# An empty first turn of the expert loop, transposes in two parts, no unused work at the tail, and 22 instead of 28 shared gate/up steps

## The chip, the cores and the metric

One core of one Trainium2 chip runs the whole program; the other cores are idle. The metric is the device time of one execution in microseconds (us), lower is better. All arithmetic is in float32. The engines are PE (matrix products; PEld is its loading of weights), DVE (elementwise), ACT (activation functions and copies), POOL (here mostly the starting of gathers and scatters) and SP (the starting of plain DMA transfers).

## The reference

The block has two halves over 1024 tokens of width 1024: a mixer (short convolution beside an RWKV-7 recurrence) and a mixture of experts. The change is in the second half, of which this is the core:

```python
def moe_ffn(xn, router_w, router_b, gu_w, gu_b, dn_w, dn_b):
    logits = xt @ router_w + router_b
    top_vals, top_idx = lax.top_k(logits, 4)          # of 32 experts
    gates = jax.nn.softmax(top_vals, axis=-1)
    ...                                               # tokens sorted by expert
    def expert_block(args):
        xb, e = args
        h = xb @ gu_w[e] + gu_b[e]                    # gate and up, 1024 -> 2 x 1024
        x_glu = jnp.minimum(h[:, 0::2], 7.0)
        x_lin = jnp.clip(h[:, 1::2], -7.0, 7.0)
        act = x_glu * jax.nn.sigmoid(1.702 * x_glu) * (x_lin + 1.0)
        return act @ dn_w[e] + dn_b[e]                # down, 1024 -> 1024
    ...                                               # times the gate, added at the token's row
y = rms_norm(h + moe_ffn(rms_norm(h, norm_ffn_w), ...), norm_final_w)
```

## The kernel before

The first half and the routing take the first 740 us of the span. The routing writes a list of tokens for each expert and, with DVE at L1484, a table `size_i` of one number for each expert: 1, 2 or 3, for up to 128, 144 or 160 tokens. Each engine then goes round its own loop over the experts; the engines meet only at semaphores. The order within an engine is the order of the code; nothing reorders it.

PE's loop is `expert_pe` (L2238 on). It is software pipelined by one expert: turn `t` finishes the down product of expert `t - 1` and then makes the gate/up product of expert `t`. In one turn PE issues:

- `down_first` (L2202): the down product is made with seven block products in place of eight (a Strassen scheme), in sums of quarters, and `down_first`, `down_second` and `down_third` are its stages. All share the helper `both` (L2194). DVE reads what a stage left in PSUM before the next stage may write there: L1549 (`y_first`) reads after `down_first`, and `down_second` waits for it; L1554 reads after `down_second`, and `down_third` waits for it.
- `transpose_tokens` (L2223 on): eight transposes of 128x128 (L2229) of the gathered tokens of the next expert into PSUM banks 4 and 5, and two (L2235) of the pieces of tokens 128 to 159 into bank 7. ACT copies these three to SBUF (`copy_xT`, L1019 and L1022) and counts `s_xe`.
- `down_second`, then `down_rest` (L2177, 32 small products for tokens 128 to 159) if the size is over 1, or `no_rest` (L2184, one dummy product) if it is 1, then `down_third`, of which the last part writes bank 6.
- `gate_up` (L2145): 128 steps, each one product of a 128x128 weight tile with 128, 144 or 160 tokens. In the code stand three copies: 100 steps with 160 tokens, 100 with 144, 122 with 128. Steps 100 to 121 stand once, with 160 tokens, for both larger sizes, and the last 6 once for all sizes. `WIDE` sets the first number. A float32 product of this kind shows as two matmul records and two weight loads in the trace.

The sizes reach PE's sequencer (the part of the engine that runs branches and hands matmuls to a queue) by `value_load`: register operations, a TENSOR_LOAD from `size_i`, and more register operations (L2240).

Before the loop PE issues 8 products on constants (`WARM`, L2131). After it the last expert's down product is made without the Strassen scheme (`down_half`, L2162), with a last set of transposes between its halves, of tokens that no expert uses. In step with that, POOL starts a last gather of such tokens (`gather(E, 0, E)` in `last_rows_out`) ahead of the load of the last expert's rows from `sum_s`, and ACT copies the transposes (`copy_xT(E)`).

In the tail DVE (`last_expert_dve`) takes the last expert's rows, adds the bias (L1594, L1595), makes from ACT's sums of squares (L1049) the scale of every token (L1597, ACT L1059, L1600), scales five of the eight output tiles (L1577; ACT scales three), and then handles the down product of the last expert. SP writes the eight tiles to `out` (L600), and when all have landed POOL scatters the last expert's rows over them (L753, L756).

`rounds` calls `expert_pe(0)`; its branch with a loop variable `r` is for experts with more than 160 tokens and is not entered with these inputs.

## Time and profile before

| | |
|---|---|
| median of 3 runs | 2271.7 us (2269.38 to 2271.95) |
| profiled execution, its own time | 2272.49 us |
| its span, first to last instruction | 2270.4 us |
| mean granted clock of PE | 0.990 |
| PE busy | 2200.7 us (97%) |
| DVE, ACT, POOL busy | 1259.6, 478.9, 350.2 us |
| the chain that ended last, by engine | PE 92%, DMA 3%, issue 2%, DVE 2% |
| of it the gate/up products (L2145) | 41% |
| of it the down products (L2194) | 17% |
| turns with a down part in the loop | 31 |
| transfers of kind "instruction" of 16 KB (queue q8) | 37, 0.61 MB |

The busy shares say that PE is hardly ever idle; the chain of waits goes through PE for 92% of the span. The granted clock is 1 at TensorE's full speed and 0.5 at half of it. "issue" as the cause of an idle time means that the engine waited for nothing that the profile shows. Queue q8 carries code to an engine.

### The profile page before, as it was taken

Reading aid. Unit: us, or ns where it says so; the run is one execution under the profiler, and the core shown is the slowest. Engines: PE = TensorE matmul, PEld = TensorE weight load, DVE = VectorE, ACT = ScalarE, POOL = GpSimd, SP = SyncE. Lnnn points to the kernel's source line nnn. Section 1 sums busy time; section 2 is a strip of 40 time slices with the busy share of each in tenths; the row PEclk is TensorE's granted clock in tenths of the full one; section 3 lists DMA queues with packets and bytes.
Section 4 is the critical chain, followed back from the end, with each engine's and each line's share of the span. In section 5 each row is a group of like instructions: output and inputs, shape, how many; then the busy total and the mean of one; then the engine's idle time right before and its main releaser. Section 6 shows DMA issues by size and latency. Waiting matters only on the chain.

```text
span 2270.4 us, 49537 instructions
## 1 busy us (share of the span) xinstructions
PE 2200.7 (97%) x19222; PEld 1600.0 (70%) x19223; DVE 1259.6 (55%) x2504; ACT 478.9 (21%) x988; POOL 350.2 (15%) x360
## 2 busy tenths in 40 slices
PE   8999998899999998999999999999999999999997
PEld 3444444888445776888678877788777887788775
DVE  6466533455434455556655665556655665556664
ACT  3233001444333111111111111111111111111113
POOL 0000001121022211111112211122111221121112
PEclk9999999999998999999999999999999999999998
DMA  3111112333533767888878988689877998679987
GB/s 143 50 60 47 51 61 64 96 104 123 192 131 104 310 254 279 304 301 309 333 272 298 344 303 308 253 324 340 307 301 263 333 350 325 254 292 334 349 300 260
DMA packets 120628, 535.01 MB, mean 236 GB/s; under 512 B 27795, under 2 KB 61735, under 8 KB 87776
## 3 DMA queue, kind: packets, MB, share of 16 engines
q1 hardware_dynamic: 98416, 489.30, 56.2%
q0 software_dynamic: 22160, 44.98, 7.8%
q8 instruction: 37, 0.61, 0.1%
q14 instruction: 15, 0.12, 0.0%
HBM read 485.24 MB, written 40.05 MB: 231 GB/s over the span
## 4 chain that ended last, share of the span: by engine, by line
PE 92%; DMA 3%; issue 2%; DVE 2%; POOL 0%; ACT 0%; SPq 0%; POOLq 0%; DVEq 0%
PE ps L2145 41%; PE ps L2194 17%; PE ps L1654 9%; PE ps L1752 5%; PE ps L2025 5%; PE ps L2177 2%; PE ps L1851 2%; PE ps L2229 1%; PE ps L1701 1%; PE ps L1860 1%; DMA idx_g<-list_s 1%; PE ps L1833 1%; PE ps L1865 1%; DMA arena<-xn_s,idx_g 1%; PE ps L1953 1%
## 5 line engine op out<-in xcount | busy, mean ns | idle before, releaser
L2145 PE MATMUL ps<-arena 128*128 128x128 f32 (+2 forms) x8192 | 994.2, 284 | 10.3 <-issue 8.9
L2145 PEld LDWEIGHTS ps<-arena 128*128 128x128 f32 x8192 | 986.2, 192 | 22.9 <-issue 21.2
L2194 PE MATMUL ps<-arena 128*64 128x512 f32 x1984 | 393.3, 544 | 9.9 <-DVE arena L1554 9.7
L1508 DVE TENSOR_TENSOR arena<-arena 128x1024 f32<-128x1024 f32 x248 | 294.3, 1217 | 0.0
L2194 PEld LDWEIGHTS ps<-arena 128*64 128x64 f32 x1984 | 134.2, 137 | 218.9 <-issue 193.9
L1495 DVE TENSOR_SCALAR arena<-ps,arena 128x160 f32<-128x160 f32 x256 | 97.9, 382 | 321.3 <-PE ps L2145 320.0
L1027 ACT ACTIVATE arena<-arena 128x160 f32<-128x160 f32 x256 | 86.1, 336 | 815.9 <-DVE arena L1495 815.9
L1654 PE MATMUL ps<-arena 128*128 128x512 f32 x448 | 195.7, 594 | 0.0
L730 POOL DMA_INDIRECT sum_s<-arena,idx_s x31 | 51.5, 1662 | 851.9 <-ACT arena L1042 851.9
L1654 PEld LDWEIGHTS ps<-arena 128*128 128x128 f32 x448 | 84.5, 190 | 109.4 <-issue 109.4
L1752 PE MATMUL ps<-arena 128*128 128x512 f32 x280 | 120.6, 592 | 0.8 <-ACT arena L871 0.8
L2025 PE MATMUL ps<-arena 128*128 128x512 f32 x256 | 113.7, 594 | 0.0
L1499 DVE SCALAR_TENSOR_TENSOR arena<-arena 128x160 f32<-128x160 f32 x256 | 83.3, 325 | 49.1 <-ACT arena L1027 48.1
L1752 PEld LDWEIGHTS ps<-arena 128*128 128x128 f32 x280 | 53.1, 190 | 68.1 <-issue 68.1
L1496 DVE TENSOR_SCALAR arena<-ps,arena 128x160 f32<-128x160 f32 x256 | 95.8, 374 | 0.0
L714 POOL DMA_INDIRECT arena<-xn_s,idx_g x33 | 39.6, 1200 | 351.7 <-DMA idx_g<-list_s 336.1
L1502 DVE TENSOR_TENSOR arena<-arena 128x160 f32<-128x160 f32 x256 | 83.2, 325 | 8.8
L2025 PEld LDWEIGHTS ps<-arena 128*128 128x128 f32 x256 | 47.6, 190 | 55.2 <-issue 54.9
L1554 DVE TENSOR_TENSOR arena<-ps,arena 64x512 f32<-64x512 f32 x31 | 21.2, 684 | 108.7 <-PE ps L2194 108.7
L1042 ACT ACTIVATE arena<-arena,idx_s 128x512 f32<-128x512 f32 x62 | 44.8, 722 | 145.1 <-DVE arena L1567 140.2
L1851 PE MATMUL ps<-arena 64*64 64x64 f32 x1328 | 56.9, 224 | 7.7 <-issue 5.3
L1561 DVE TENSOR_TENSOR arena<-ps,arena 64x512 f32<-64x512 f32 x31 | 21.2, 684 | 77.1 <-PE ps L2194 77.1
(280 smaller groups left out, 2088.6 us busy)
## 6 DMA issues: line engine op xcount, KB each, us to landing
arena<-gu_w SPq DMA_DIRECT2D x128, 2048.0 KB, 11.5
arena<-dn_w SPq DMA_DIRECT2D x128, 1024.0 KB, 11.2
arena<-dn_b SPq DMA_DIRECT2D x32, 512.0 KB, 15.4
arena<-w_in_t SPq DMA_DIRECT2D x26, 512.0 KB, 3.2
arena<-arena SPq DMA_DIRECT2D x50, 256.0 KB, 2.7
arena<-w_out SPq DMA_DIRECT2D x2, 2048.0 KB, 7.9
arena<-x SPq DMA_DIRECT2D x8, 512.0 KB, 5.1
xn_s<-arena SPq DMA_DIRECT2D x8, 512.0 KB, 2.8
```

What stands on the lines that cost most here:

```text
L1027: nc.scalar.activation(sgm[f % 2], gt[f % 2], ACT.Sigmoid, scale=ALPHA).then_inc(s_gs, 1)
L1495: nc.vector.tensor_scalar(gt[b], ps[:, b, 0:C], g0, LIMIT, ALU.add, ALU.min).then_inc(s_g1, 1)
L1496: nc.vector.tensor_scalar(lt[b], ps[:, b, C:2 * C], g1, LIMIT + 1, ALU.add, ALU.min).then_inc(s_gd, 1)
L1499: nc.vector.scalar_tensor_tensor(out=lt[b], in0=lt[b], scalar=1 - LIMIT, in1=sgm[b], op0=ALU.max, op1=ALU.mult).then_inc(s_l1, 1)
L1502: nc.vector.tensor_tensor(actT[:, f, :], lt[b], gt[b], ALU.mult).then_inc(s_act, 1)
L1508: nc.vector.tensor_tensor(dst[:, w, :], a[:, w, :], b[:, w, :], op).then_inc(s_ds, 1)
L1654: last = nc.tensor.matmul(ps[:, bank + h, :], win[:, slot, kt * P:(kt + 1) * P], xnT[:, kt, h * HALF:(h + 1) * HALF], start=kt == 0, stop= ...
L1752: last = nc.tensor.matmul(ps[:, bank, :], weights[:, k * P:(k + 1) * P], tokens[:, k, :], start=start and k == 0, stop=stop and k == K2 - ...
L1851: last = nc.tensor.matmul(out_at(s, 0, h if l == 0 else 1 - h, r), MTs[s][own(h), r, :], Tst[s][own(h), r, :], start=True, stop=True)
L2025: last = nc.tensor.matmul(ps[:, 2 * (t % 2) + h, :], (mix_conv, mix_y)[part][:, k, t * P:(t + 1) * P], (woA, woB)[part][:, k, h * HALF:(h ...
L2145: last = nc.tensor.matmul(ps[:, f % 2, k * C:k * C + size], wslot[u][:, kt, o:o + P], xT[:, kt, 0:size], start=kt == 0, stop=kt == KT - 1, ...
L2194: last = nc.tensor.matmul(ps[rows, bank, 0:width], acts[:, k, :], weights[:, k, :], start=first and k == 0, stop=k == K2 - 1, skip_group_c ...
```

## The change

It consists of five edits.

1. The wait for the sizes (`s_sz`) stands ahead of PE's loop, and the loop has 33 turns. In the first, `k = 0`, the number of the expert is read from a new row `size_i[:, ROUNDS, :]` (DVE fills it with 0 to 31 at L1461 of the new file), the whole part with transposes and down product is skipped, and the size read for the gate/up product is 0, so that this is skipped too. Turn `k` from 1 on is the old turn `k - 1`. The expert's number is read from the table in every turn, and the size for the down part is read ahead of `down_first` and not after it.
2. `transpose_tokens`: part 0 makes six of the eight transposes and stands ahead of `down_second`; part 1 makes two and those of the pieces and stands behind it.
3. `down_third`: its last part writes bank 5 in place of bank 6, waits for ACT's copy of bank 5 instead of DVE's reading of bank 6, and the wait for `a_all` moves to its start.
4. `WIDE = END - 22`: 22 steps are shared between the sizes, 28 before. The copies for 160 and 144 tokens have 106 steps each.
5. Tail: no last gather, no last transposes, no `copy_xT(E)`. DVE's L1594 and L1595 stand behind the scaling of the tiles.

```diff
@@ POOL, ACT
             def last_rows_out():
                 n = E - 1
-                gather(E, 0, E)
                 pool.wait_ge(s_sc, 32 * n)
...
-                copy_xT(E)
                 act.wait_ge(s_sq2, 2 * TT)
@@ DVE
-            nc.vector.memset(size_i[:, :, :], 0)
+            ch.link(nc.vector.memset(size_i[:, :, :], 0))
...
                 if t == 0:
+                    ch.link(nc.vector.tensor_copy(size_i[:, ROUNDS, 1:E + 1], iexp))
...
-            nc.vector.tensor_copy(size_i[:, :, 1:E + 1], size_f).then_inc(s_sz, 1)
+            nc.vector.tensor_copy(size_i[:, 0:ROUNDS, 2:E + 2], size_f).then_inc(s_sz, 1)
...
-                dve.wait_ge(s_ls, 16 * TT * TOPK + 32)
-                dve.wait_ge(s_db, 16 * (PIECES + 1) * (n + 1))
-                dve.wait_ge(s_is, 32 * n + 32)
-                nc.vector.scalar_tensor_tensor(out=rows, in0=dnb, scalar=gate, in1=rows, ...)
-                nc.vector.scalar_tensor_tensor(out=rows2, in0=dnb2, scalar=gate2, in1=rows2, ...)
                 dve.wait_ge(s_sq2, 2 * TT)
...
                 for t in range(ACT_TILES, TT):
                     scaled_tile(t)
+                dve.wait_ge(s_ls, 16 * TT * TOPK + 32)
+                dve.wait_ge(s_db, 16 * (PIECES + 1) * (n + 1))
+                dve.wait_ge(s_is, 32 * n + 32)
+                ch.link(nc.vector.scalar_tensor_tensor(out=rows, in0=dnb, scalar=gate, in1=rows, ...))
+                ch.link(nc.vector.scalar_tensor_tensor(out=rows2, in0=dnb2, scalar=gate2, in1=rows2, ...))
@@ PE
-            WIDE = END - 3 * KT - 4
+            WIDE = END - 22
...
             def down_third(n, m, q, o):
                 pe.wait_ge(s_ds, 8 * q + 8 + 8)
+                pe.wait_ge(s_as, 5 * q + 5 + 5)
                 pe.wait_ge(s_xe, 3 * m + 4)
                 pe.wait_ge(s_ye, o + 7)
                 both((2, a_sum, d_dif, False), (4, a22, d_all, True), True)
-                pe.wait_ge(s_as, 5 * q + 5 + 5)
-                pe.wait_ge(s_ye, o + 8)
-                both((6, a_all, d22[:, :, 0:PW], True), (6, a_all, d22[:, :, PW:HALF], True), True)
+                pe.wait_ge(s_xe, 3 * m + 5)
+                both((5, a_all, d22[:, :, 0:PW], True), (5, a_all, d22[:, :, PW:HALF], True), True)

             def transpose_tokens(m, part):
...
-                for kt in range(4 * part, 4 * part + 4):
+                for kt in range(6 * part, 6 + 2 * part):
...
+                def down_and_transposes(turn, size, n, m):
+                    o, q = five(n, r), summed(n, r)
+                    with pe.If(turn > 0):
+                        down_first(n, q, o)
+                    transpose_tokens(m, 0)
+                    with pe.If(turn > 0):
+                        down_second(n, q, o)
+                    transpose_tokens(m, 1)
+                    with pe.If(size > 1):
+                        down_rest(n, o, q)
+                    with pe.If(size == 1):
+                        no_rest(o)
+                    with pe.If(turn > 0):
+                        down_third(n, m, q, o)
+
+                pe.wait_ge(s_sz, 2)
+                first = isinstance(r, int)
+                with pe.Fori(0, E + 1) as k:
+                    if first:
+                        turn = pe.value_load(size_i[0:1, ROUNDS, bass.ds(k, 1)], min_val=0, max_val=E - 1)
+                        n, m = turn - 1, turn
+                        with pe.If(k > 0):
+                            down_and_transposes(turn, size_at(k), n, m)
+                        need = size_at(k + 1)
...
                     with pe.If(need == 3):
                         gate_up(n + 1, m + 1, SIZES[2], range(0, WIDE))
...
                 if isinstance(r, int):
-                    n, m = E - 1, E
-                    size = size_at(E)
+                    n = E - 1
+                    size = size_at(E + 1)
                     down_half(n, 0)
-                    for part in range(2):
-                        transpose_tokens(m, part)
                     with pe.If(size > 1):
```

The order of PE's instructions at the head of the loop, before: the branch back leads to these rows (`down_w12_11`, `act_sums` and the like are the semaphores waited for).

```order
L2246 COMPARE_AND_BRANCH
L2202 ISA
L2203 ISA [waits down_w12_11]
L2204 ISA [waits act_sums]
L2205 REGISTER_ALU [waits down_weight_sums]
L2194 MATMUL ps<-arena 64x512 [waits dn_read]
```

And now, from the same place to the first matmul of `down_first`:

```order
L2266 TENSOR_LOAD size_i
L2266 ISA x2
L2268 COMPARE_AND_BRANCH
L2244 ISA
L2244 TENSOR_LOAD size_i
L2244 ISA x2
L2249 COMPARE_AND_BRANCH
L2205 ISA
L2206 ISA [waits down_w12_11]
L2207 ISA [waits act_sums]
L2208 REGISTER_ALU [waits down_weight_sums]
L2197 MATMUL ps<-arena 64x512 [waits dn_read]
```

Two reads from the table stand between the branch back and the first matmul, where none stood before; the old read of the size came behind `down_first`.

PE around `down_second`, before:

```order
L2229 MATMUL ps<-cst,arena 128x128 [waits tokens_gathered]
L2229 MATMUL ps<-cst,arena 128x128 x7
L2235 MATMUL ps<-cst,arena 128x128 [waits pieces_gathered]
L2235 MATMUL ps<-cst,arena 128x128
L2251 COMPARE_AND_BRANCH
L2209 ISA
L2210 ISA [waits act_sums]
L2211 ISA [waits down_weight_sums]
L2212 REGISTER_ALU [waits down_w21]
L2194 MATMUL ps<-arena 64x512 [waits dn_read]
L2194 MATMUL ps<-arena 64x512 x7
```

And now:

```order
L2232 MATMUL ps<-cst,arena 128x128 [waits tokens_gathered]
L2232 MATMUL ps<-cst,arena 128x128 x5
L2252 COMPARE_AND_BRANCH
L2212 ISA
L2213 ISA [waits act_sums]
L2214 ISA [waits down_weight_sums]
L2215 REGISTER_ALU [waits down_w21]
L2197 MATMUL ps<-arena 64x512 [waits dn_read]
L2197 MATMUL ps<-arena 64x512 x7
L2252 UNCONDITIONAL_BRANCH
L2232 MATMUL ps<-cst,arena 128x128 x2
L2239 MATMUL ps<-cst,arena 128x128 [waits pieces_gathered]
```

Four of the ten transposes have moved from ahead of `down_second` to behind it.

DVE in the tail, from the last weighting of a tile on, before:

```order
L1585 TENSOR_TENSOR arena<-arena 128x1024 [waits h_squared]
L1594 SCALAR_TENSOR_TENSOR arena<-arena,idx_s 128x1024 [waits scatter_list_in,dn_bias_in,lists_written_then_sums_of_rows_in]
L1595 SCALAR_TENSOR_TENSOR arena<-arena,idx_s 128x256
L1597 TENSOR_SCALAR stat<-stat 128x8 [waits h_squared]
L1600 RECIPROCAL stat<-stat 128x8 [waits h_root]
L1577 SCALAR_TENSOR_TENSOR arena<-arena,stat 128x1024 [waits y_scaled_then_rstd]
```

And now:

```order
L1588 TENSOR_TENSOR arena<-arena 128x1024 [waits h_squared]
L1595 TENSOR_SCALAR stat<-stat 128x8 [waits h_squared]
L1598 RECIPROCAL stat<-stat 128x8 [waits h_root]
L1580 SCALAR_TENSOR_TENSOR arena<-arena,stat 128x1024 [waits y_scaled_then_rstd]
L1580 SCALAR_TENSOR_TENSOR arena<-arena,stat 128x1024 x4
L1606 SCALAR_TENSOR_TENSOR arena<-arena,idx_s 128x1024 [waits scatter_list_in,dn_bias_in,lists_written_then_sums_of_rows_in]
L1607 SCALAR_TENSOR_TENSOR arena<-arena,idx_s 128x256 [waits dve_step]
```

The instruction that waits for the last expert's rows no longer stands ahead of the scaling of the tiles.

## Rows read from the trace of the kernel before

**Rows 1.** PE's waits: engine, line, releaser; us in total, times, longest us.

```profile
PE ps L2194 <- DVE arena L1554: 9.7, 16, 0.6
```

**Rows 2.** PE in order of time: start us, us, what, idle time before it.

```profile
742.63 1.04 PE L2229 MATMUL ps<-cst,arena 128*128 128x128 f32 x8
...
745.33 27.43 PE L2145 MATMUL ps<-arena 128*128 128x160 f32 x200 [1.45 <-ACT arena L1019]
775.90 9.54 PE L2145 MATMUL ps<-arena 128*128 128x160 f32 x56 [3.14 <-issue]
...
802.69 35.04 PE L2145 MATMUL ps<-arena 128*128 128x160 f32 x256
...
857.21 30.77 PE L2145 MATMUL ps<-arena 128*128 128x128 f32 x256 [2.17 <-issue]
...
906.13 30.71 PE L2145 MATMUL ps<-arena 128*128 128x128 f32 x256 [3.58 <-issue]
...
951.35 32.37 PE L2145 MATMUL ps<-arena 128*128 128x144 f32 x256
...
1050.58 29.14 PE L2145 MATMUL ps<-arena 128*128 128x128 f32 x256
```

**Rows 3.** Windows: busy time by engine, granted clock, DMA share, GB/s.

```profile
732.60:738.80 6.20, 6.20 (x9) 2.58 (x10) 5.20 (x28) 0.00 (x0) 3.77 (x4) 0.50 0.62 201
776.30:779.70 3.40, 3.40 (x15) 3.40 (x15) 0.00 (x0) 0.00 (x0) 0.00 (x0) 0.50 0.73 308
```

**Rows 4.** DMA queues, 900 to 935 us: transfers, MB, share.

```profile
q8 instruction: 5, 0.08, 1.2%
```

**Rows 5.** DMA queues, 935 to 2235 us: the last row; q8 has none.

```profile
q0 software_dynamic: 16802, 32.60, 10.6%
```

**Rows 6.** PE's sequencer by line: count, ns min/median/max, first and last start.

```profile
L2261 PEldq COMPARE_BRANCH  x35: 66/208/5523, 741.2 to 2209.0; - x35
L2264 PEldq COMPARE_BRANCH  x1: 3585/3585/3585, 853.3 to 853.3; - x1
L2264 PEldq COMPARE_BRANCH  x1: 4782/4782/4782, 901.0 to 901.0; - x1
L2240 PEldq FUSED_REGOPS  x2: 51/101/151, 852.3 to 852.8; - x2
```

**Rows 7.** DVE writing the sizes, in order of time.

```profile
738.26 0.39 DVE L1484 CAST size_i<-arena 128x224 int32<-128x224 f32 x1
```

**Rows 8.** The matmul forms of L2145: busy us, mean ns.

```profile
L2145 PE MATMUL ps<-arena 128*128 128x144 f32 x2400 | 297.2, 287 | 0.0
```

**Rows 9.** PE and DVE in a turn of size 1, in order of time.

```profile
940.35 1.09 PE L2229 MATMUL ps<-cst,arena 128*128 128x128 f32 x8
940.47 0.68 DVE L1549 TENSOR_TENSOR arena<-ps,arena 64x512 f32<-64x512 f32 x1 [1.02 <-PE ps L2194]
...
941.59 0.20 PEld L2194 LDWEIGHTS ps<-arena 128*64 128x64 f32 x4 [0.17 <-issue]
...
945.29 0.68 DVE L1554 TENSOR_TENSOR arena<-ps,arena 64x512 f32<-64x512 f32 x1 [3.48 <-PE ps L2194]
...
946.03 5.38 PE L2194 MATMUL ps<-arena 128*64 128x512 f32 x32 [0.61 <-DVE arena L1554]
```

**Rows 10.** The head of the last loop turn: sequencer's lines, then PE's matmuls.

```profile
L2205 PEldq ALU_OP  x31: 36/36/36, 783.8 to 2194.8; - x31
...
2196.30 3.65 PE L2194 MATMUL ps<-arena 128*64 128x512 f32 x16
```

**Rows 11.** The tail: ACT in order of time, then three links of the chain.

```profile
2242.66 1.06 ACT L1049 ACTIVATE arena<-arena 128x1024 f32<-128x1024 f32 x1
...
2246.04 1.29 DVE arena L1594
...
2248.32 0.07 DVE arena L1577
...
2256.18 5.72 DMA out<-arena
```

More of the change, by code:

```diff
@@ L1590, in last_expert_dve @@
                         weighted_tile(f - KT + ACT_TILES)
-                dve.wait_ge(s_ls, 16 * TT * TOPK + 32)
-                dve.wait_ge(s_db, 16 * (PIECES + 1) * (n + 1))
-                dve.wait_ge(s_is, 32 * n + 32)
-                nc.vector.scalar_tensor_tensor(out=rows, in0=dnb, scalar=gate, in1=rows, op0=ALU.mult, op1=ALU.add)
-                nc.vector.scalar_tensor_tensor(out=rows2, in0=dnb2, scalar=gate2, in1=rows2, op0=ALU.mult, op1=ALU.add)
                 dve.wait_ge(s_sq2, 2 * TT)
@@ L1603, in last_expert_dve @@
                     scaled_tile(t)
+                dve.wait_ge(s_ls, 16 * TT * TOPK + 32)
+                dve.wait_ge(s_db, 16 * (PIECES + 1) * (n + 1))
+                dve.wait_ge(s_is, 32 * n + 32)
+                ch.link(nc.vector.scalar_tensor_tensor(out=rows, in0=dnb, scalar=gate, in1=rows, op0=ALU.mult, op1=ALU.add))
+                ch.link(nc.vector.scalar_tensor_tensor(out=rows2, in0=dnb2, scalar=gate2, in1=rows2, op0=ALU.mult, op1=ALU.add))
                 dve.wait_ge(s_par, (2 + PIECES) * 16)
```

31 lines of the change are left out of this document (16 added, 15 removed).

## The prediction

> **What bounds the kernel now.** The first view is the page's busy time: PE is busy for 97% of the span, and the chain that ended last lies on it for 92%. So nothing gains time but what shortens PE's own stream, or the tail behind it, where others take over. The second view is the list of PE's waits. In the expert loop only one of them comes from another engine regularly: `down_third` waits 0.6 us for DVE's L1554, 16 times, 9.7 us in all [rows 1]. The third view is PE in order of time [rows 2]. It shows three gaps before gate/up products, of 3.14, 2.17 and 3.58 us, put down to "issue": no engine released PE there. They stand where the sequencer jumps to a copy of the gate/up code, and the sequencer's own rows show what they are: three branches that took 5523, 3585 and 4782 ns where the middle one takes 208 ns [rows 6]. Part of that is hidden by matmuls already queued. The code queue q8 is active at these places (5 transfers from 900 to 935 us) and has no transfer at all in the 1300 us from 935 to 2235 [rows 4, 5]. So the loop's code is fetched in the first four turns and stays.
>
> A gap costs more than itself. Behind it PE runs at a granted clock of 0.50 for some 3.4 us [rows 3]. By the gate/up products around it: turn 0 took 3.14 + 1.93 us too much (27.43 + 3.14 + 9.54 against 35.04 for the same size), turn 2 took 2.17 + 1.63 (30.77 against 29.14 for the same size), turn 3 took 3.58 + 1.57 (30.71 against 29.14) [rows 2]. Together 14.0 us.
>
> The Trainium skill (Runtime: NRT & Kernel Launch, Instruction fetch mechanics) says that code is prefetched in sequence in blocks of 16 KiB, and that a taken branch out of the window held waits for a DMA. The trace agrees on the size and the stall (0.08 MB in 5 transfers, branches of 3.6 to 5.5 us); the page's window of two blocks it contradicts, since a loop with three copies of the products runs for 1300 us without a transfer.
>
> **The change, part by part.** The sum is made against the profiled execution's own 2272.49 us, which is 0.8 us above the median of the runs.
>
> *The empty first turn, its cost.* The sizes are written at 738.26 + 0.39 = 738.65 us [rows 7]. Only then does the sequencer enter the loop. One read of the table with the taken branch behind it takes 1.0 us (852.3 to 853.3 [rows 6]). The empty turn reads twice, which brings it to about 740.6. Its branches then lead to the head of the 144 copy, to the head of the 128 copy and to the shared steps, none of which has been fetched. No row shows such a series; each of the three branches seen took 3.6 to 5.5 us, mean 4.6. Three are 13.9 us, bounds 10.8 and 16.6. From 754.5 the end of the turn and the head of the next (two reads, a few branches) are 2.9 us more, and the first transposes start at some 757.4 to 758 against 742.63 before [rows 2]. The warming products end by then at 742.7, so nothing covers this: the first gate/up product is late by 15.5 us (12 to 18.5).
>
> *Its second cost, the clock.* After such a pause PE restarts at 0.50. Before, PE got its full clock back only 6.2 us after it became busy at 732.6 [rows 3]. That is one to two of the periods that cost 1.6 to 1.9 us each above, but the transposes and the wait for ACT's copy (2.7 us, 742.63 to 745.33) lie in it. I take 2.3 us, bounds 0.5 and 3.4.
>
> *Its gain.* If the empty turn leaves every block in place, the three gaps go with their slow periods: 14.0 us. What is late there next is nothing: the products before and behind a gap are on PE itself.
>
> *22 shared steps.* A record at 160 tokens takes 35.04/256 = 0.137 us, one at 144 (32.37 - 56 x 0.137)/200 = 0.1235 us [rows 2]. Six steps are 12 records, and 2400/200 = 12 experts have this size [rows 8]: 12 x 12 x 0.0134 = 1.9 us gained. The other sizes don't change.
>
> *The split transposes, size 1.* Now the ten transposes run from 940.35 to 941.59, and DVE's L1549, for which `down_second` must wait, ends at 940.47 + 0.68 = 941.15 [rows 9]: it is covered with 0.4 us to spare. With six transposes (6/10 of 1.24 is 0.75) the transposes end at 941.1 and `down_second` starts when DVE releases it, at 941.21: 0.38 us earlier. Behind it the four moved transposes (0.5 us) fall into the 0.61 us in which PE waited for L1554. So each of the 16 turns with that wait [rows 1] is shorter by 0.38 us: 6.1 us. Not 9.7, because a new wait of 0.1 us ahead of `down_second` takes the place of the old one, and one more change between kinds of product costs PE something.
>
> *The split, larger sizes.* In the other 15 of 31 turns `down_rest` already fills the place behind `down_second`. There the new wait (0.1 us) and the additional change of kind (below 0.1) are a pure loss: 0.15 x 15 = 2.3 us, bounds 0 and 3.
>
> *Two reads at the head of the loop.* In the last turn L2205, the last operation before the products, stands at 2194.8, so that the first matmul of `down_first` can be handed on at 2194.9; PE gets to it at 2196.30 [rows 10]. The queue covers 1.4 us. The two reads with their branches add 0.8 + 0.8 us, less what the old head's compare took, so 1.5 to 1.6. That is 0.2 us more than the cover. Behind a larger size the cover is 1.5 us (L2205 at 783.8, products until 785.4 [rows 2, 10]), and 0.05 us is left. Over 16 and 15 turns this is 4.0 us, bounds 0 and 10 (if each register operation is 0.1 us longer than assumed it is 0.3 us in every turn). Behind the stalled sequencer nothing else is queued, and DVE and ACT wait for `down_first` in any case.
>
> *Bank 5 in place of 6, the earlier wait for `a_all`.* In turn 0 all transposes and ACT's three copies take 2.7 us together (742.63 to 745.33 [rows 2]); the moved transposes start at 944.8 and the last part of `down_third` comes only behind its first, some 4 us later. DVE makes `a_all` before L1554, for which PE waits anyway. Nothing.
>
> *The additional copy and the linked memset on DVE* are 0.2 us each, early in the routing, where DVE waits for PE's output product. Nothing.
>
> *Tail.* ACT's last square ends at 2243.7, but the scale is made only behind L1594, which waited for the last rows until 2246.04 and takes 1.29 us with L1595 behind it: the scale's first step comes at 2247.7 and the first tile at 2248.3. Without this the step can start at 2243.9; ACT has to load its table for the root before it goes on (I take 1.3 us, an estimate), so that the first tile is scaled at about 2245.6. The transfers of the tiles, of which the last is in the chain for 5.72 us, and POOL's scatter behind it move with it [rows 11]: 2.7 us, bounds 1 and 3. The rows' own work now stands behind the tiles on DVE but ends 0.6 us before the last tile has landed. The ten transposes left out (1.2 us of PE) and POOL's gather are off this chain.
>
> *Sum:* +15.5 + 2.3 - 14.0 - 1.9 - 6.1 + 2.3 + 4.0 - 2.7 = -0.6 us against 2272.49, which makes 2271 for the median. I see the change as a trade in which the first turn's gain is paid for in front.
>
> **The rivals.**
>
> *Faster.* Branches into missing code cost 3.6 us each (as the middle one did), the slow clock falls on the transposes, and the queue covers the two reads. That is 3.1 + 1.8 + 4.0 us less: 2262. For it speaks that DVE, ACT and POOL ask for little at that time; against it, two of three such branches were longer.
>
> *Slower, one mechanism: the empty turn pays for blocks that do not stay.* The copy for size 1 was fetched at 853.3 and missing again at 901.0, one turn later [rows 6]. Code brought by a jump seems to displace other code until the blocks lie in order. The empty turn comes to them only by jumps. If they are displaced again, the gaps of the first turns come back while the front is paid: +14.0, 2285. It decides at the first turn with a new size. Against it: the empty turn touches the blocks in rising order, as turn 3 did, behind which nothing was fetched any more.
>
> *Slower by much: the loop's code no longer stays at all.* Then each of 31 turns has a gap like those of rows 2 with its slow period, 4.7 us: +146, 2417. By the same page of the Trainium skill PE's instruction memory is 128 KiB, 2048 instructions in blocks of 256; with one block fetched ahead 1792 stay, and 1803 is more. But that count takes every product as four instructions, and eight transposes show as eight records [rows 2], half of what it assumes; ten transposes are 20 fewer, 1783. I give it 5 in 100.
>
> *Slower by its costs:* branches of 5.5 us, two slow periods, 0.35 us at each head: +2.7 + 1.1 + 6 = 2281.
>
> **How the numbers follow.** Forecast 42 in 100, with its own range 2266 to 2276; faster rival 25; blocks that do not stay 15; costs 13; overflow 5. A measurement of this kernel tells a difference from about 0.2%, 4.5 us. Below 2267.2 lie the faster rival and the edge of the forecast, 0.28; above 2276.2 the three slower ones, 0.32; between them 0.40. The range that leaves 2 in 10 outside is 2262 to 2286: it ends at the faster rival's centre, takes in the one where blocks do not stay, and leaves out the overflow.
>
> **What would show it.** Right: the first transposes at 756 to 759 us; no gap above 1 us before any later gate/up product; q8 quiet from the second turn on; the wait for L1554 gone from PE's list, and in its place 0.1 us before `down_second`; idle time of 0.1 to 0.3 us by "issue" before `down_first`; turns of size 1 shorter by 0.2 us and of size 2 the same to 0.1; the tiles scaled 2.7 us nearer to the last gate/up product. Wrong: transposes before 752 (branches cheap), code transfers in the middle of the loop, or turns of size 1 that are not shorter.

## The result, and the profile after

The changed kernel takes 2278.6 us (median of 8 runs, 2277.3 to 2280.8) against 2271.8 us of the kernel before beside it (8 runs, 2269.4 to 2274.7): ratio 1.0029, 95% interval 1.0020 to 1.0038. It is slower by 6.8 us. The forecast was 2271 us, a change of -0.6. The time lies in the forecast's range, 2262 to 2286 us, but the likeliest outcome named was no change beyond 0.2%, and the measured loss is clear of its interval.

In the profile after, line numbers have moved: gate/up 2145 is now L2148, the down products' `both` 2194 is L2197, the transposes 2229 are L2232 and 2235 are L2239, the dummy product 2184 is L2187; on DVE 1549 is L1552, 1554 is L1557 and the tiles' scaling 1577 is L1580; ACT's copy 1019 is L1025. The profiled execution took 2278.67 us with a span of 2276.9 (before 2272.49 and 2270.4).

PE in order of time (start us, us, what, idle time before it), from the warming products to the third gate/up product:

```profile
731.76 10.12 PE L2134 MATMUL ps<-cst 128*128 128x512 f32 x16
764.11 1.97 PE L2232 MATMUL ps<-cst,arena 128*128 128x128 f32 x8 [22.23 <-issue]
765.87 0.64 PE L2239 MATMUL ps<-cst,arena 128*128 128x128 f32 x2
767.02 37.44 PE L2148 MATMUL ps<-arena 128*128 128x160 f32 x256 [0.52 <-ACT arena L1025]
...
821.96 35.04 PE L2148 MATMUL ps<-arena 128*128 128x160 f32 x256
```

These answer to [rows 2]. The first gate/up product starts at 767.02 instead of 745.33, behind 22.23 us in which PE has nothing, put down to "issue": no engine released it, and its own sequencer was late. The product then takes 37.44 us where the next of its size takes 35.04. Its first microseconds run at half clock, by these windows (start and end, length, busy time of PE, PEld, DVE, ACT and POOL, granted clock, DMA share, GB/s):

```profile
764.00:767.00 3.00, 2.39 (x10) 2.00 (x10) 0.00 (x0) 1.46 (x4) 0.00 (x0) 0.50 0.00 0
767.00:770.00 3.00, 2.98 (x11) 2.98 (x12) 0.00 (x0) 1.27 (x1) 2.31 (x3) 0.50 0.27 42
```

No later gate/up product has a gap. The sequencer's rows (count, ns min/median/max, first and last start) show what filled PE's idle time. They answer to [rows 6]:

```profile
L2275 PEldq COMPARE_BRANCH  x1: 5743/5743/5743, 740.2 to 740.2; - x1
```
```profile
L2278 PEldq COMPARE_BRANCH  x1: 7557/7557/7557, 746.0 to 746.0; - x1
```
```profile
L2281 PEldq COMPARE_BRANCH  x1: 7384/7384/7384, 753.6 to 753.6; - x1
```

These are the three branches of the empty turn, each over one of the three copies. They take 20.7 us together, where the forecast had 13.9. Behind them q8, the code queue, is quiet until the tail, as forecast: from 765 to 2245 us the DMA queues of the trace are these three, and q8 is not among them (transfers, MB, share):

```profile
q1 hardware_dynamic: 46904, 413.46, 71.3%
q0 software_dynamic: 18848, 36.72, 10.4%
q14 instruction: 1, 0.01, 0.0%
```

In a turn of size 1 the wait for L1557 has gone, and a short one for L1552 stands before `down_second`. These lines answer to [rows 9]:

```profile
907.33 0.87 PE L2232 MATMUL ps<-cst,arena 128*128 128x128 f32 x6
907.44 0.68 DVE L1552 TENSOR_TENSOR arena<-ps,arena 64x512 f32<-64x512 f32 x1 [1.18 <-PE ps L2197]
...
908.18 0.20 PEld L2197 LDWEIGHTS ps<-arena 128*64 128x64 f32 x4 [0.21 <-DVE arena L1552]
...
911.88 0.68 DVE L1557 TENSOR_TENSOR arena<-ps,arena 64x512 f32<-64x512 f32 x1 [3.10 <-PE ps L2197]
...
912.62 5.38 PE L2197 MATMUL ps<-arena 128*64 128x512 f32 x32
```

The six transposes end at 908.2, and so does the wait for L1552 (908.12); L1557 ends at 912.56, and PE goes on at 912.62. From one gate/up product to the next such a turn takes 43.43 us, against 43.65 before.

The tail, three links of the chain that ended last, which answer to [rows 11]:

```profile
2252.98 0.07 DVE arena L1580
...
2260.86 5.69 DMA out<-arena
...
2268.77 0.98 POOL out L759
```

The first tile is scaled 34.32 us behind the start of the last gate/up product (2218.66), before 37.44 (2248.32 - 2210.88): 3.1 us gained. But from the last gate/up product to the end of the span only 1.3 us are gained (59.54 before, 58.21 after). The rest is in POOL's last long instruction, a drain. No view of the profile lists it; these are the trace's instruction records (start in us, length):

```
before  2268.32 GpSimd DRAIN 1872 ns      span 2270.4
after   2272.56 GpSimd DRAIN 4077 ns      span 2276.9
```

Term by term, in us:

| term | forecast | trace after |
|---|---|---|
| first gate/up product later | +15.5 | +21.7 |
| its slow clock | +2.3 | +2.4 |
| gaps removed | -14.0 | -14.0 |
| 22 shared steps, 12 turns (32.21 for 32.37) | -1.9 | -1.9 |
| split, 16 turns of size 1 | -6.1 | -6.1 (0.38 each, isolated below) |
| split, 15 larger turns | +2.3 | +3.0 (0.20 each, isolated below) |
| reads at the head | +4.0 | +3.8 (0.17 in 16 turns, 0.07 in 15) |
| tail | -2.7 | -1.3 |
| sum | -0.6 | +7.6 (spans: +6.5) |

One turn of size 1 before took 44.37 instead of 43.65 for a reason not looked into; its 0.7 us are in the difference between the sum and the spans. So one term is off by 6.2 us, one by 1.4, and the rest by less than 1.

### The profile page after: what moved, and what is told of

Its sections match the earlier page's. It is cut to its first block, busy times and chain, and to the rows that moved or that the text cites. A ratio compares the mean times of both kernels' runs of the same rounds, so it can differ in the third digit from the quotient of the medians.

```text
span 2276.9 us, 49684 instructions
## 1 busy us (share of the span) xinstructions
PE 2204.9 (97%) x19212; PEld 1597.3 (70%) x19213; DVE 1261.2 (55%) x2505; ACT 480.5 (21%) x985; POOL 345.8 (15%) x356
## 3 DMA queue, kind: packets, MB, share of 16 engines
q0 software_dynamic: 21904, 44.98, 7.8%
## 4 chain that ended last, share of the span: by engine, by line
PE 93%; DVE 3%; issue 2%; DMA 1%; ACT 0%; SPq 0%; POOL 0%; DVEq 0%; POOLq 0%; ACTq 0%
PE ps L2148 41%; PE ps L2197 17%; PE ps L1657 9%; PE ps L1755 5%; PE ps L2028 5%; PE ps L2180 2%; PE ps L1854 2%; PE ps L2232 2%; PE ps L1704 1%; PE ps L1863 1%; DVE arena L1511 1%; PE ps L1836 1%; PE ps L1868 1%; DMA arena<-sum_s 1%; PE ps L1956 1%
## 5 line engine op out<-in xcount | busy, mean ns | idle before, releaser
L2148 PEld LDWEIGHTS ps<-arena 128*128 128x128 f32 x8192 | 981.8, 191 | 12.8 <-issue 11.9
L2148 PE MATMUL ps<-arena 128*128 128x128 f32 (+2 forms) x8192 | 989.5, 284 | 0.5 <-ACT arena L1025 0.5
L2197 PE MATMUL ps<-arena 128*64 128x512 f32 x1984 | 393.3, 544 | 2.1
L2197 PEld LDWEIGHTS ps<-arena 128*64 128x64 f32 x1984 | 135.2, 137 | 213.4 <-issue 191.2
L1022 ACT COPY arena<-ps 128x512 f32<-128x512 f32 x64 | 37.5, 586 | 254.8 <-PE ps L2232 254.8
L2232 PEld LDWEIGHTS ps<-cst,arena 128*128 128x128 f32 x256 | 27.6, 143 | 73.4 <-issue 72.5
L1557 DVE TENSOR_TENSOR arena<-ps,arena 64x512 f32<-64x512 f32 x31 | 21.2, 684 | 96.0 <-PE ps L2197 96.0
## 6 DMA issues: line engine op xcount, KB each, us to landing
arena<-w_out SPq DMA_DIRECT2D x2, 2048.0 KB, 12.2
```

The costliest lines, as they stand in the source:

```text
L2148: last = nc.tensor.matmul(ps[:, f % 2, k * C:k * C + size], wslot[u][:, kt, o:o + P], xT[:, kt, 0:size], start=kt == 0, stop=kt == KT - 1, ...
L2197: last = nc.tensor.matmul(ps[rows, bank, 0:width], acts[:, k, :], weights[:, k, :], start=first and k == 0, stop=k == K2 - 1, skip_group_c ...
L2232: last = nc.tensor.transpose(ps[:, 4 + kt // 4, kt % 4 * P:(kt % 4 + 1) * P], xg[:, kt * P:(kt + 1) * P], ident)
```

## The experiments

The kernel before took 2271.8 to 2274.7 us (medians) beside the various runs. Comparisons therefore go by the ratio to the runs beside each; an expectation in us is to be divided by 2271.8. Where a table row says "one run" there is no interval, and only the trace is read.

| run | median us | ratio, 95% interval |
|---|---|---|
| e1 no empty turn | 2260.7 | 0.9949 (0.9936 to 0.9962) |
| e2 empty turn before the sizes | 2274.5 | 1.0005 (0.9996 to 1.0014) |
| e3 size read later | 2276.7 | 1.0020 (1.0011 to 1.0029) |
| e4 tail alone | 2272.2 | 0.9996 (0.9987 to 1.0005) |
| e5 loop head of before | 2264.5 | 0.9962 (0.9948 to 0.9976) |
| e6 split alone | 2270.3 | 0.9981 (0.9972 to 0.9990) |
| e7 spaced jumps | 2306.0 | one run |
| e8 8 shared steps | 2601.9 | 1.1442 (1.1427 to 1.1458) |
| e9 weights held | 2270.4 | 0.9985 (0.9976 to 0.9994) |
| e10 held, early, read later | 2265.2 | 0.9958 (0.9946 to 0.9971) |
| e11 no empty turn, read later | 2257.6 | 0.9937 (0.9921 to 0.9953) |
| e12 e11 with the last gather | 2259.6 | 0.9941 (0.9927 to 0.9955) |
| e13 e5 with the wait outside | 2263.0 | 0.9953 (0.9940 to 0.9966) |
| e14 e13 moved by two | 2262.3 | one run |
| e15 e13 with a read at the head | 2257.8 | one run |

**e1, without the empty turn.**

```
-                with pe.Fori(0, E + 1) as k:
+                with pe.Fori(1 if first else 0, E + 1) as k:
```

> The kernel after, but its loop starts at the first real turn, so that the empty turn is never run; all other edits stay. Theory (the empty turn costs more than it saves: its three branches took 5.7, 7.6 and 7.4 us, the first gate/up product stood 21.7 us later and lost 2.4 us to the half clock, and 14.0 us of later gaps went): the first product stands at 745 to 747 us, the gaps of the first turns are back with some 14 us, and the time is 2278.6 - 21.7 - 2.4 + 14.0 = 2268.5 us (2265 to 2272), below the kernel before. Rival (the loss is in the turns or the tail, and the empty turn paid for itself): 2278 us or more.

The direction was right and the gain larger: 0.9949 is 2260.2 on the scale of the expectation, 8 us below its centre and 5 below its range. These are PE's gate/up products of the first turns (the list ends at 910 us, inside the last one):

```profile
748.39 29.06 PE L2148 MATMUL ps<-arena 128*128 128x160 f32 x212 [2.13 <-issue]
779.11 6.24 PE L2148 MATMUL ps<-arena 128*128 128x160 f32 x44 [1.66 <-issue]
...
802.81 35.04 PE L2148 MATMUL ps<-arena 128*128 128x160 f32 x256
...
857.66 5.51 PE L2148 MATMUL ps<-arena 128*128 128x128 f32 x47 [2.29 <-issue]
863.57 23.90 PE L2148 MATMUL ps<-arena 128*128 128x128 f32 x209 [0.41 <-issue]
...
901.75 8.42 PE L2148 MATMUL ps<-arena 128*128 128x128 f32 x73
```

Two gaps are back, with less lost to them: the first product is 1.9 us too long instead of 5.1 before (36.96 from start to end against 40.11). The third, before the product at 901.75, has not come back. So even the 14.0 us of removed gaps were not all the empty turn's own: 5.2 us of them go without it (e13 to e15 bear on why). The empty turn costs 24 us (21.7 + 2.4) and saves 5 us against e1, or 9 of the gaps of before.

**e2, the empty turn before the sizes are known.**

```
-                pe.wait_ge(s_sz, 2)
                 first = isinstance(r, int)
...
                         with pe.If(k > 0):
+                            pe.wait_ge(s_sz, 2)
                             down_and_transposes(turn, size_at(k), n, m)
```

> The kernel after, with PE's wait for the sizes moved from ahead of the loop to behind the empty turn. The sequencer then enters the loop at some 732.7 us instead of 737.8 while the eight warming products still run. Theory (the three branches have a fixed length of about 20.7 us from the moment the sequencer enters, and nothing else holds the first product): the first product 5.1 us earlier, near 762 us, time 2273.5 us (2272 to 2275). Rival (the fetches are slowed while PE and the queues are busy, or the first product waits for its tokens): the branches get longer and the time stays at 2277 to 2279 us.

The gain is the one that the theory had, but not by its terms. From the start of the warming products to the first gate/up product it is 30.1 us (730.18 to 760.27), where after has 35.3 (731.76 to 767.02): 5.2 less, and 1.0005 against 1.0029. The three branches were not of fixed length. The first of them fell from 5.74 to 2.48 us:

```profile
L2275 PEldq COMPARE_BRANCH  x1: 2483/2483/2483, 735.8 to 735.8; - x1
```

SP requests the last weights of the first expert only at 736.8 us here, behind this branch's start. The other two, behind that request, took 8.08 and 7.73 us. And the jump over the turn's body, 0.46 us in after, now takes 3.79 with a code fetch in it. The longer jump and the shorter first branch cancel, 3.3 us each.

**e3, one read later.**

```
                     with pe.If(turn > 0):
                         down_first(n, q, o)
+                    size = size_at(at)
                     transpose_tokens(m, 0)
```

> The kernel after, with one of the two table reads at the head of the loop put back behind the first down product. Theory (the 3.8 us of idle time ahead of the 31 first down products in the trace after come from these reads, whose sequencer time is 0.2 us more than the queue covers): with 0.5 to 0.6 us less at the head all 31 gaps go, and the time falls by 3.8 us to 2274.8 us (2274 to 2276). Rival (the gaps come from something else, a taken branch or the longer loop, or the read now delays the transposes): within 1 us of 2278.6.

In after the 31 first down products start 3.8 us later in sum, counted from the last record of the gate/up product before, than in the kernel before; here it is 0.0. The time shows it less sharply (1.0020 against 1.0029, intervals overlapping). With the heads clean, the split can be read off alone: a turn of size 1 takes 43.27 us (before 43.65), of size 2 49.66 (49.62, with 0.16 less in its products), of size 3 52.48 (52.28). That is -0.38 and +0.20.

**e4, the tail alone**, on the kernel before:

```
-                gather(E, 0, E)
...
-                copy_xT(E)
...
-                nc.vector.scalar_tensor_tensor(out=rows, in0=dnb, scalar=gate, in1=rows, op0=ALU.mult, op1=ALU.add)
...
                 for t in range(ACT_TILES, TT):
                     scaled_tile(t)
+                ch.link(nc.vector.scalar_tensor_tensor(out=rows, in0=dnb, scalar=gate, in1=rows, op0=ALU.mult, op1=ALU.add))
...
-                    for part in range(2):
-                        transpose_tokens(m, part)
```

> The kernel before with the edits of the tail alone (no transposes, copy and gather for a turn that has no expert, and the rows' own work behind the scaled tiles). In the trace after, the tiles are scaled 3.1 us nearer to the last gate/up product, but POOL's drain at the very end took 4.08 us where it took 1.87 before. Theory (the tiles' gain is real and the drain's length is chance or hangs on something outside the tail): 2271.8 - 3.1 = 2268.7 us (2268 to 2269.5). Rival (the longer drain comes with the edit, since POOL reaches it earlier after its transfers): 2270.9 us (2270 to 2271.5), with a drain of about 4 us in the trace.

The rival came about: ratio 0.9996, a gain of about 1 us with zero inside the interval, and a drain of 4077 ns.

**e5, the loop head of before** (the kernel before with the split, the 22 steps and the tail), and **e6, the split alone.**

> The kernel before with the split transposes, the 22 shared steps and the tail edits, and neither the empty turn nor its table reads: the loop's head and its branches are those of before. In the run without the empty turn only two of the three gaps of before came back (with branches of 4.05 and 3.64 us); the third, at the fourth turn (3.58 + 1.57 us), did not. Theory A (that gap went with the 22 shared steps, which lengthen the copies): it is gone here too, all 31 heads have no idle time, and the time is 1.4 us below that run's 2260.7: 2259.3 us (2258 to 2261). Theory B (it went with the loop's new head): the gap is back, 2264.4 us (2263 to 2266).

> The kernel before with the split transposes and the product in bank 5 alone. With the idle time at the heads gone, turns of size 1 took 43.27 us against 43.65 before, turns of size 2 took 49.66 against 49.62 with 0.16 less in the products, and size 3 took 52.48 against 52.28. Theory (the split gains 0.38 in each of 16 turns and loses 0.2 in each of 15, gaps as before): 2271.8 - 6.1 + 3.0 = 2268.7 us (2267.5 to 2270). Rival (the split itself moves code so that a gap of the first turns goes or comes): 5 us to either side of this.

e5 came out by theory B: the gap of the fourth turn is there, 3.57 us with a branch of 4843 ns at 900.2. e6 came out as expected (0.9981, expected 0.9986), with the three gaps of before.

**e7, a pause between the jumps**, behind the first and the second, and 26 shared steps in place of 22 to make room:

```
+                        with pe.If(k == 0):
+                            with pe.Fori(0, 8):
+                                size_at(0)
```

> The kernel after with a pause in the empty turn behind its first and its second jump (eight table reads in a small loop, some 6 us each), and 26 instead of 22 shared steps to make room. Theory (a jump that comes right behind the one before waits for the read-ahead of the block just entered: in the trace after the fetch began 3.2 to 3.4 us behind the branch, in two of three of the kernel before 0.7 and 1.0 us): the second and third jump fall from 7.5 us to 3.6 to 4.8 us each, and the first product comes 12 - 6 = 6 us later than in after. Rival (a jump into missing code in this state takes 7.5 us whatever went before): branches of 7.4 us or more, the first product 12 us later.

Neither theory holds in full. The sequencer's rows:

```profile
L2281 PEldq COMPARE_BRANCH  x1: 6702/6702/6702, 756.5 to 756.5; - x1
```
```profile
L2287 PEldq COMPARE_BRANCH  x1: 3587/3587/3587, 771.6 to 771.6; - x1
```
```profile
L2281 PEldq COMPARE_BRANCH  x1: 4677/4677/4677, 935.7 to 935.7; - x1
```

The first gate/up product came 14 us later than in after (781.19). The second jump still took 6.70 us, the third fell to 3.59. Each now had one code fetch in it, where each had two in after. Two later turns missed a block in spite of the empty turn (886.3, 3501 ns, and 935.7): there the rival that I had given 15 in 100 took place, the empty turn paying for blocks that do not stay. So spacing takes away the second fetch, but it isn't all that sets the price: between 760 and 771 us something else had changed. What changes there is the load on the DMA engines: in the 3 us from the second jump's start the DMA share is 1.03, in those from the third's 0.03. These are windows of 3 us from the start of a branch, first of after (a share can be a little over 1, since a transfer counts whole in the window in which it starts):

```profile
740.20:743.20 3.00, 1.68 (x4) 0.38 (x2) 0.00 (x0) 0.00 (x0) 2.39 (x3) 1.00 0.89 344
746.00:749.00 3.00, 0.00 (x0) 0.00 (x0) 0.00 (x0) 0.00 (x0) 0.00 (x0) 0.50 1.00 419
753.60:756.60 3.00, 0.00 (x0) 0.00 (x0) 0.00 (x0) 0.00 (x0) 1.35 (x2) 0.50 1.02 429
```

and of the kernel before, its branches of 5523, 3585 and 4782 ns:

```profile
770.20:773.20 3.00, 2.56 (x19) 2.32 (x18) 2.58 (x6) 0.34 (x1) 0.00 (x0) 1.00 1.10 409
853.30:856.30 3.00, 1.74 (x18) 0.86 (x12) 2.85 (x5) 0.36 (x1) 0.00 (x0) 1.00 0.12 22
901.00:904.00 3.00, 1.55 (x16) 0.73 (x12) 2.89 (x6) 0.55 (x1) 0.00 (x0) 1.00 0.29 52
```

The longest branch of the kernel before is the one under full load, and the empty turn puts all three there: at 738.2 us SP requests the first expert's last 8 MB of weights, and from 740.2 to 761 us the DMA share in after is 0.97.

**e9, the weights held**, which tests this:

```
+            sp.wait_ge(s_xt, 1)
             for u in (2, 3):
                 sp.dma_start(wslot[u], weights_of(0, u)).then_inc(s_wt[u], 16)
             down_weights(0)
```

> The kernel after, with the 8 MB of weights that SP otherwise requests at 738 us (the first expert's third and fourth gate/up tile and its down weights) held until PE's first transposes are done. Theory (the length of a branch into missing code hangs on what the DMA engines carry: at a DMA share of 0.00 to 0.04 the fetch began 0.7 to 1.0 us behind the branch and a branch with one fetch took 3.6 us, with two 4.8; at a share near 1.00 it began 2.7 to 4.2 us behind it and the branches took 5.5 to 7.6): the empty turn's branches take 3.6 + 4.8 + 4.8 = 13.2 us instead of 20.7, the fetches begin about 1 us behind each, the first product stands 7.5 us earlier, and the time is 2271 us (2270 to 2273). Rival (the price comes from jumps that follow one another closely, or from the state of the code memory, not from the load): branches as in after, time 2278 us or, with the weights late, more.

Windows from the start of its three branches, then the branches (the first is the longest of L2276):

```profile
747.40:750.40 3.00, 1.07 (x3) 0.19 (x1) 0.00 (x0) 0.00 (x0) 2.39 (x3) 1.00 0.03 4
750.00:753.00 3.00, 0.00 (x0) 0.00 (x0) 0.00 (x0) 0.00 (x0) 2.39 (x3) 0.59 0.12 14
755.10:758.10 3.00, 0.00 (x0) 0.00 (x0) 0.00 (x0) 0.00 (x0) 1.35 (x2) 0.50 0.13 12
```
```profile
L2276 PEldq COMPARE_BRANCH  x2: 71/1306/2541, 747.4 to 764.9; - x2
```
```profile
L2279 PEldq COMPARE_BRANCH  x1: 5011/5011/5011, 750.0 to 750.0; - x1
```
```profile
L2282 PEldq COMPARE_BRANCH  x1: 4682/4682/4682, 755.1 to 755.1; - x1
```

The three branches take 12.2 us instead of 20.7. The fetches begin 0.6 and 0.7 us behind the last two instead of 3.4 and 3.2, and the first branch's own fetch had begun just before it. From the warming products to the first gate/up product it is 26.8 us instead of 35.3, and the ratio falls from 1.0029 to 0.9985. That is 2268.4 us on the scale of the expectation, 1.6 us below its range, which the interval covers. (The trace is of e9's slowest execution, 2277.5 us, which is why the front is measured from the warming products.) That the load makes the branches long is shown: nothing but the time at which the weights are requested was changed.

The Trainium skill (DMA: Bandwidth & Descriptors, Queues, rings and completion order) says that each DMA engine takes turns between the queues it has work for, a packet at a time. The runs agree in kind: at full load a code fetch begins up to 4.2 us late.

**e8, 8 shared steps.** `WIDE = END - 8` on e5: 1825 instructions in the loop.

> The kernel of the first run of this call with 8 instead of 22 shared steps. The loop then has 1825 instructions by count of the program, and reaches into an eighth block of 256. Theory A (seven blocks and the one fetched ahead are all that stay): each of 31 turns has a code fetch and a gap of 1.9 to 3.6 us with its slow period, at least 31 x 3 = 93 us more, over 2350 us. Theory B (eight blocks stay as well): 14 steps less shared are 28 products in 12 turns at 0.0134 us, 4.5 us less than the first run of this call.

Theory A holds, and the loss is far over its bound: 14.4%. The page of the profile counts (transfers, MB, share)

```profile
q8 instruction: 206, 3.38, 0.6%
```

where after has 30, and a turn has some two misses, not one. A stretch of PE shows the gaps:

```profile
1580.89 4.35 PE L2147 MATMUL ps<-arena 128*128 128x160 f32 x16 [7.05 <-issue]
...
1636.94 6.56 PE L2196 MATMUL ps<-arena 128*64 128x512 f32 x16 [5.11 <-issue]
...
1664.23 31.95 PE L2147 MATMUL ps<-arena 128*128 128x128 f32 x256 [10.12 <-issue]
```

So the limit that the rival "the loop's code no longer stays" spoke of exists. By count of the compiled programs it lies between 1775 instructions, the loop of after, and 1825. The Trainium skill's figure (Runtime: NRT & Kernel Launch, Instruction fetch mechanics) of 2048 instructions in blocks of 256 agrees, if one block is kept for fetching ahead; its window of two blocks does not.

This run also makes a table possible. It has all branches of PE's sequencer over 1.5 us in the 17 traces in which a code fetch began, 121 in all and 60 of them from e8. They are sorted by the DMA share from 0.5 us before to 3.0 us behind the branch's start (code transfers left out) and by the number of fetches in the branch. The delay is that of the first fetch; it and the length of the branch are given as mean and extremes in us:

```
DMA share   fetches   n    delay               branch
below 0.1      1      31   1.07 (0.92-1.56)    3.60 (3.29-3.92)
below 0.1      2      11   0.69 (0.44-0.98)    4.82 (4.68-5.01)
0.1 to 0.8     1      18   1.10 (0.56-1.44)    3.64 (3.25-3.88)
0.1 to 0.8     2      10   2.02 (1.82-2.19)    6.09 (5.94-6.28)
above 0.8      1      24   2.55 (0.96-4.20)    5.10 (3.72-6.70)
above 0.8      2      27   3.22 (1.60-4.23)    7.40 (6.43-8.32)
```

Load makes a branch longer on average, but it doesn't fix the length: with one fetch at full load it was 3.72 us at the least and 6.70 at the most.

**e10 and e11, the combinations.**

> The kernel after with three changes at once: the weights held as in the run before this, PE's wait for the sizes behind the empty turn (which took 5.2 us from the start in its own run), and the size read behind the first down product (3.8 us). Theory (the three are independent): 2278.6 - 7.5 - 5.2 - 3.8 = 2262.1 us (2261 to 2264), with no gap in any turn. Rival (they overlap: entering earlier meets other DMA traffic, or the held weights come too late for an earlier first product): 2265 to 2270 us.

> The kernel after without the empty turn and with the size read behind the first down product. Theory (the 1.4 us of idle time at the heads that were left without the empty turn go, and only the two gaps of the first and third turn stay): 2260.7 - 1.4 = 2259.3 us (2258 to 2261). Rival (with the read moved the third gap of the kernel before returns, as in the run whose loop head was that of before): 2264.5 us.

e10: 0.9958 is 2262.3 us on the scale of the expectation, as the theory had it, though not by its terms. Entering early gained 2.4 us here and not 5.2 (24.5 us from the warming products to the first gate/up product, e9 26.8). The jump over the turn's body met missing code in both (3.25 us here, 3.79 in e2). The difference is in the first of the three branches: without the load there was nothing left to gain on it, and it rose from 2.54 us in e9 to 3.38. e11: 0.9937 (expected 0.9945), the lowest ratio of the runs with an interval, with two gaps and no delay at the heads.

**e12, the last gather put back.** POOL's `gather(E, 0, E)` stands again in e11, and PE and ACT only count for it.

> The kernel without the empty turn and with the size read later (2257.6 us, 0.9937), and with POOL's last gather of a turn without expert put back: two list transfers and two indirect ones on POOL's queue, without PE's transposes and ACT's copy of them. POOL's drain at the very end took 4077 ns in every trace with the tail edit (seven of them) and 1872 ns in both without it. Theory (the drain's length hangs on how many transfers POOL has posted, and the gather left out is what lengthened it): 1872 ns here, and the time 2.2 us less, ratio 0.9928. Rival (the drain's length comes with the shorter way from the last tile to POOL's scatter, or with another edit of the tail): 4077 ns, ratio 0.9937.

The drain is back at 1872 ns, by the theory. The expected gain in time is not seen: the time from the last gate/up product to the end is 57.4 us (2194.34 to 2251.7) against 58.8 in e11 (2194.58 to 2253.4) in the traces, but the runs don't resolve it (0.9941 and 0.9937, where 0.9928 was expected). So the longer drain came with the gather left out. Why, no run shows. POOL's queue had 22160 packets with the short drain, 21904 with the long one.

**e13, e14, e15, the gap of the fourth turn.** e13 has the wait for the sizes ahead of the loop; e14 adds to it three `pe.sem_inc(s_pe_apart, 1)` at the loop's head, e15 instead `size_at(turn)`, unused.

> The kernel with the loop head of before (split transposes, 22 shared steps and tail edits; 0.9962), with PE's one wait for the sizes moved from inside the loop, ahead of the read that chooses the copy, to ahead of the loop. Its two sisters without the empty turn, whose head reads a table and which wait outside, have no gap in the fourth turn; it has one (branch of 4.84 us, 3.5 + 1.6 us of PE). Theory A (the wait's place decides, since the sequencer then doesn't stand in the middle of the loop's code while blocks are fetched ahead): the gap of the fourth turn goes, ratio 0.9962 - 5.1/2272 = 0.9940. Theory B (the reads at the head or the loop's start value decide): the gap stays, ratio 0.9962.

> The kernel of the run with the sizes awaited outside (three gaps: 1.75, 2.3 and 3.6 us), with three semaphore increments that nobody needs at the loop's head. They move all of the loop's code back by two places and read nothing. Theory A (what decides whether the fourth turn misses its block is where the code lies, or how long it is): the gap of the fourth turn goes and the time is 5.1 us less than that run's. Theory B (a read of the table at the head decides): the gap stays.

> The same kernel with one table read at the loop's head that nobody uses. It moves the code back by the same two places. Theory A (the place of the code): the gap of the fourth turn goes, as in the run beside it. Theory B (the read): it goes here only. If it stays in both, the loop's start value or a third place is what the kernels without that gap have and these have not.

The fourth turn's product in e13, e14 and e15 (the first two lists end at 930 us, inside it):

```profile
903.36 26.85 PE L2147 MATMUL ps<-arena 128*128 128x128 f32 x213 [3.48 <-issue]
```
```profile
904.28 25.95 PE L2147 MATMUL ps<-arena 128*128 128x128 f32 x230
```
```profile
899.07 29.14 PE L2147 MATMUL ps<-arena 128*128 128x128 f32 x256
```

The gap stays in e13 and goes in both others. So neither the wait's place nor the read decides; what e14 and e15 share is code that lies two instructions further back. The times alone would not say it: e13's interval takes in both of its theories, and e14's one time, 2262.3 us, is hardly below e13's 2263.0. In e14's trace the warming products start 2.6 us later, and the first gate/up product takes 39.4 us instead of 36.8, which hides the gain. The other traces fit. By the compiled programs the first gate/up copy starts at the same place in the five kernels with this gap (before, e4, e5, e6, e13) and two or three instructions further back in the five without an empty turn that don't have it (e1, e11, e12, e14, e15). The length of the loop doesn't decide: it is 1743 instructions in before and 1767 in e5, both with the gap. Which edge of a block this moves what across was not found.

## Why the prediction was wrong

**The step that failed** is the price of the three branches in the empty turn: "No row shows such a series; each of the three branches seen took 3.6 to 5.5 us, mean 4.6. Three are 13.9 us, bounds 10.8 and 16.6." They took 20.7, and the first transposes stood at 764.11 us, outside the 756 to 759 that the prediction had named as its sign. The mechanism was right (three jumps into code not fetched, nothing to cover them, blocks that stay); I took the mean of three branches without asking what made one of them 5.5 and another 3.6. The windows of the kernel before held the answer: a DMA share of 1.10 at the one and 0.12 at the other. The empty turn falls into a time when the weights load at full rate, a share of 0.97 from 740.2 to 761 us in after. And it makes jumps follow one another, so that two of three carry two fetches. By the table's last row and the one above it, which I had only afterwards, two of 7.4 and one of 5.1 are 19.9. With that the front costs 21.5 and the sum gives 2277 us. e9 shows the load's part by taking it away; e7 bears on the second fetch. My argument for the faster rival, that DVE, ACT and POOL ask for little at that time, looked at the wrong engines.

**The gain of the empty turn** was 14.0 us as forecast, but credited wrongly: the fourth turn's 5.2 us go with the place of the code (e14, e15), which the change moves by itself. That the sum came out at 14.0 is luck in this part. What I called a trade was none: e1 is 0.8% faster than after.

**The clock** (+2.4 for +2.3): right. **The 22 steps**: 1.9 as forecast. **The split**: -0.38 in 16 turns is exact; +0.20 for +0.15 in 15. **The reads at the head**: 3.8 for 4.0, and moving one read takes them away (e3). **The tail**: the tiles came 3.1 us sooner (2.7 forecast); what was missing is an instruction behind the last one I looked at, POOL's drain, longer by 2.2 us (e4, e12).

**The rivals.** "Costs", 2281 us, was the nearest and right in kind, with the wrong parts: it had branches of 5.5 us where they took 6.9 on average, and heads of 0.35 us where they took 0.07 to 0.17. (31 heads of 0.35 us are 6.9 us over the forecast's 4.0, not 6, which makes it 2282.) Blocks that do not stay came about in e7 alone, overflow in e8. The overflow rival's count was 8 too high: the compiled loop of after has 1775 instructions, not 1783, which changes nothing in its outcome.

## What to carry to other kernels

A jump into code that is not there costs more while the DMA engines are loaded, so fetch code ahead of need while they are idle, or not at all. Look at the DMA share of the very microseconds into which a step is moved, not at where a similar step stood. An empty turn has to be paid for in full where nothing runs beside its jumps. No run here made it pay: with the weights held and the loop entered early it gave 0.9958 (e10), and without it, with the same later read, 0.9937 (e11). Before paying for fetched code, try the loop a few instructions further along and look whether a miss goes.

## What the hardware showed unexpectedly

A branch into missing code took 3.6 us on average (one fetch) or 4.8 (two) with idle DMA engines and up to 8.3 with busy ones, in 121 cases. A loop of 1775 instructions had no fetch in 1480 us; the kernel with one of 1825 had 206 in all and lost 14%. With two more instructions at a loop's head a miss of 5 us was gone, in one trace each of e14 and e15. And POOL's final drain took exactly 1872 or 4077 ns, the short one in the three traces with POOL's last gather (before, e6, e12), the long one in the fourteen without.
